# Transformer layer on one NeuronCore: TensorE makes each attention score one head further ahead

## What is computed

```
for i in blocks of 128 queries:                      # 8 row blocks
    s_loc = q_i . k[i-1, i, i+1] * scale, masked to |distance| <= 128
    s_ctx = q_i . k_ctx * scale
    p = softmax([sink, s_ctx, s_loc])
    o_i = p[ctx] @ v_ctx + p[loc] @ v[i-1, i, i+1]   # for each of 8 query heads
```

## Time and profile before

| | |
|---|---|
| median of 3 runs | 1198.11 us (1193.68 to 1208.54) |
| profiled execution | 1199.23 us, span 1197.4 us |
| PE busy | 1138.2 us (95%) |
| DVE busy | 936.9 us (78%) |
| ACT busy | 573.9 us (48%) |
| mean granted clock of TensorE | 0.981 |
| head groups (first turn to end of the last values) | 241.2 to 432.2 us |

### The profile page before, as it was taken

The page is one execution under the profiler, slowest core; times in us unless marked ns, Lnnn a source line. Parts: engine busy times, 40 slices in busy tenths (PEclk is TensorE's granted clock), DMA queues, the critical chain, the costliest instruction groups (busy, mean ns, idle before and its releaser), DMA issues.

```text
span 1197.4 us, 17074 instructions
## 1 busy us (share of the span) xinstructions
PE 1138.2 (95%) x5953; PEld 969.7 (81%) x5953; DVE 936.9 (78%) x1428; ACT 573.9 (48%) x981; POOL 290.2 (24%) x331
## 2 busy tenths in 40 slices
PE   7899999989898999998799999999999999999996
PEld 7778888889898887776688787878888878888885
DVE  1479988769897664469999999999999875867763
ACT  4362346756565765545444434344434444444441
POOL 2100011115455000002544545463600030000111
PEclk9999999979999999999899999999999999999998
DMA  9321555519999514212444453535333284443474
GB/s 368 132 76 62 128 102 110 114 64 223 251 264 256 151 53 158 106 69 89 155 162 152 146 175 123 175 123 175 123 122 105 88 298 159 115 115 96 119 165 69
DMA packets 103090, 171.77 MB, mean 143 GB/s; under 512 B 9322, under 2 KB 62690, under 8 KB 102004
## 3 DMA queue, kind: packets, MB, share of 16 engines
q1 hardware_dynamic: 82388, 104.70, 26.4%
q0 software_dynamic: 20640, 66.27, 23.5%
HBM read 112.21 MB, written 31.46 MB: 120 GB/s over the span
## 4 chain that ended last, share of the span: by engine, by line
PE 33%; DVE 16%; issue 8%; ACT 5%; DVEq 1%; ACTq 0%; POOL 0%
PE ps L1603 11%; PE ps L1653 6%; PE ps L1654 6%; PE ps L1655 6%; PE ps L1568 5%; DVE y L2016 4%; DVE w_op L1915 3%; DVE w_raw L1933 2%; DVE y L2012 2%; ACT w_op L1724 2%; ACT y L1804 2%; DVE u L2005 1%; DVE s_sum L1933 1%; ACT h_first L1717 0%; DVE scal L2047 0%
## 5 line engine op out<-in xcount | busy, mean ns | idle before, releaser
L1603 PE MATMUL ps<-t_op,w_op 128*128 128x512 f32 x1056 | 247.6, 390 | 3.2 <-DVE cv L2005 1.8
L1603 PEld LDWEIGHTS ps<-t_op,w_op 128*128 128x128 f32 x1056 | 197.6, 188 | 47.4 <-issue 4.3
L1603 PE MATMUL ps<-hx,w_op 128*128 128x512 f32 x792 | 192.4, 396 | 10.7 <-DVE u L2005 7.5
L1603 PEld LDWEIGHTS ps<-hx,w_op 128*128 128x128 f32 x792 | 150.8, 191 | 45.0 <-DVE u L2005 6.5
L1724 ACT ACTIVATE w_op<-w_raw 128x512 fp32r<-128x512 f32 x132 | 80.0, 623 | 199.5 <-DVE w_raw L1933 190.8
L1653 PE MATMUL ps<-dnh,ah 128*128 128x512 f32 x308 | 120.0, 390 | 1.6 <-DVE dnl L2023 1.6
L1655 PE MATMUL ps<-dnh,al 128*128 128x512 f32 x308 | 119.8, 389 | 0.0
L1654 PE MATMUL ps<-dnl,ah 128*128 128x512 f32 x308 | 119.8, 389 | 0.0
L1915 DVE TENSOR_TENSOR w_op<-w_raw,w_op 128x512 fp32r<-128x512 f32 x132 | 101.4, 782 | 10.0 <-ACT w_op L1724 8.2
L1824 ACT ACTIVATE ah<-hid 128x512 fp32r<-128x512 f32 x77 | 48.6, 632 | 116.7 <-PE ps L1655 112.7
L2023 DVE TENSOR_TENSOR al<-hid,ah 128x512 fp32r<-128x512 f32 x77 | 53.3, 692 | 48.8 <-ACT ah L1824 48.0
(11 more groups left out here) (287 smaller groups left out, 2393.3 us busy)
## 6 DMA issues: line engine op xcount, KB each, us to landing
w_raw<-in_w_up SPq DMA_DIRECT2D x44, 512.0 KB, 5.0
wm<-in_w_mod SPq DMA_DIRECT2D x32, 512.0 KB, 6.1
sums<-wm POOLq DMA_DIRECT2D x32, 512.0 KB, 8.4
wd<-in_w_down POOLq DMA_DIRECT2D x44, 256.0 KB, 3.3
w_down_sums<-wd POOLq DMA_DIRECT2D x44, 256.0 KB, 2.8
dn_raw<-w_down_sums SPq DMA_DIRECT2D x44, 256.0 KB, 2.6
hid_scratch<-hid SPq DMA_DIRECT2D x20, 512.0 KB, 4.2
hid<-hid_scratch POOLq DMA_DIRECT2D x20, 512.0 KB, 5.4
```

The lines of the kernel that those rows point to most:

```text
L1603: last = pe.matmul(bank_of(p, s), w_op[p][w][:, k, :], rows_of(p, k, v), start=(start and k == 0 and w == 0 and v == 0), stop=(k == KH - 1 ...
```

## The change

In head groups, TensorE makes the score of head hh = 4(n + 1) + j + 1 ahead of `turn(n, j)`, where it made that of head 4(n + 1) + j. So at j = 3 of group n it makes the first score of group n + 2. The very first place is as it was (two scores), the second, which was without, gets one, and groups 14 and 15 have one less and none. ScalarE's, VectorE's and the queues' lists are the same, and so are the banks and every wait inside `scores` and `turn`.

```diff
                         if (n, j) == (0, 0):
                             scores(1, 0)
-                            scores(1, 1)
-                        elif (n, j) != (0, 1) and n + 1 < NGRP and j < GQ:
-                            scores(n + 1, j)
+                        hh = GQ * (n + 1) + j + 1
+                        if j < GQ and hh < GQ * NGRP:
+                            scores(*divmod(hh, GQ))
                         turn(n, j)
```

## The result

The changed kernel took 1256.91 us (median of 4, 1254.34 to 1288.18) against 1196.36 us for the kernel before (4 runs, 1193.68 to 1208.54): ratio 1.0491, 95% interval 1.0447 to 1.0535. By the ratio it is 59 us slower, and the median lies outside the forecast range of 1211 to 1246. The highest run was a disturbed one and is left out of the ratio. The profiled execution took 1254.34 us, its span 1252.5 us.

A forecast was written before the change was run, and what follows sets the result against it. TensorE and VectorE were taken as close to full in the head groups, waiting mostly for each other. Terms of 20.6 + 1.5 + 3.5 + 3.0 = 28.6 us on 1199.23 gave 1227.8, stated as 1227.5 us, range 1211 to 1246.

The forecast's parts named there:

- That the groups are on the path, and nothing hides them: Behind the head groups TensorE runs without a gap, so a microsecond lost in them is one of the whole kernel.
- The closed chain: Head-group steps: turn, copy, exponential, score, next turn become one chain, 3.12 us against 2.23; eleven groups, +20.6 us.
- The sum of 28.6 us: Whole kernel: 20.6 us for eleven groups plus 1.5, 3.5 and 3.0 us, added to the profiled time.
- The smaller terms: Squares in groups 11 and 12 +1.5 us, groups 0 and 1 +3.5, groups 13 and 14 +3.0.
- The clock: Rival: idle of about 1.5 us per group brings half clock, 1.24 us in one step, 16 us in all; chance 0.20.
- What the profile would show: Scores (line 646) idle 40 to 50 times by about 0.9 us, once per group 1.5; VectorE's score waits near nothing.
- a shorter chain: Rival in the group steps: a step of 2.7 us, 15 us slower in all, about 1215 us; chance 0.14.
- VectorE setting the pace: Rival in the groups: the score's wait does not bite, a group takes 11.2 us, about 1187 us; chance 0.08.

The follow-up runs named there:

- The four-bank kernel: Changed kernel with four key tiles instead of five in groups 2 to 9 and scores there in four single banks: 1212.53 us, ratio 1.0118 to the kernel before.
- The kernel that keeps the full clock: Changed kernel plus 11 unread 128x256 matmuls behind turn 0 in groups 1 to 13: 1230.07 us, ratio 1.0285 to the kernel before.

## Why the prediction was wrong

- **That the groups are on the path, and nothing hides them**: right. Groups 2 to 12 lost 52.3 us and the span grew by 55.1 us.
- **The closed chain**: right, link by link (3.12 us forecast, 3.16 measured), and so was the group (14.15 against 14.25). The four-bank kernel and the one with the score behind the turn show it from two sides. The sum of 28.6 us was made for a full clock. The kernel that keeps the full clock has a profiled span 29.7 us above before's; its ratio of 1.0285 means 34 us, with an interval of 28 to 40.
- **The smaller terms**: not separable from the clock in the changed kernel. With the long idle filled, groups 0 and 1 cost 1.1 us more than before (forecast 3.5), groups 2 to 12 cost 23.7 (forecast 20.6 + 1.5) and groups 13 and 14 cost 5.9 (forecast 3.0, at most 4; the clock fell in group 14 behind an idle of 2.14 us). The total fits, in part because these misses cancel. The bounds of the terms add up to 1220 to 1233 us on the median, not to the 1218 to 1237 that the prediction gives.
- **The clock**: here the prediction failed. The sum has no term for it; it stood beside the sum as a rival of 16 us. I saw the trigger, named the place (the idle of 1.5 us behind turn 0, measured 1.55), and the price per step was right (1.24 us; measured 4.39 against 3.15). Two things were wrong. I held it unlikely, 0.20, on the argument that the turn and the score around the idle time are dense. The trace of before had no idle of that length between them, so nothing there bore the argument out, and it had a second case of the low clock that I did not use, behind an idle of 2.00 us:

```profile
362.18 1.10 PE L686 MATMUL ps<-vraw,pt 128*128 128x64 f32 x8 [2.00 <-ACT pt L989]
...
364.17 1.07 PE L674 MATMUL ps<-ident,p 128*128 128x128 f32 x4
```

And I let each idle time cost one step. The low clock did not come behind each, but where it came it lasted, once for about 31 us and once for 34 us on end: twelve steps of 4.4 us in groups 2, 3, 6, 7, 9 and 10, five more of 3.6 to 4.2 us in groups 2, 5, 6 and 9, and in groups 6 and 9 the group's end too (8.8 us from turn 3 to the next turn 0, against 4.8). That is 12 x 1.25 + 5 x 0.75 + 2 x 4.0 = 27 us. The measured price is the ratio of 1.0491 to 1.0285, 2.0% or about 25 us, where the rival had 16. Forecast and clock together, 1227.5 + 25, would have been 1253. What I had not thought of is that the short idle times, harmless alone, count beside the long one.
- The rule that I cited from the Trainium skill ("TensorE: Matmul & The Clock Gate", section on a second failure mode) describes such a case, short idle times between groups of matmuls that cycle through PSUM banks, and the trace agrees with it: clock 0.73 in the groups, and 1.00 once the long idle time in each is filled. I had weighed it by a single counterexample of 1.09 us, shorter than the idle at hand.
- **What the profile would show**: the idle before line 646 came, mostly 0.71 us (forecast 0.9) and 1.55 us, but 28 times and not 40 to 50. A group has two short ones beside the long one, not three, and at half clock TensorE's own work in a step (4.39 us) covers the chain. VectorE's waits for scores did not vanish: once TensorE is slower than VectorE, VectorE waits for it again.
- **The rivals on the other side** (a shorter chain, VectorE setting the pace) had no support: from group 1 on, no step of the changed kernel whose score has five key tiles was shorter than 3.1 us.

## What to carry to other kernels

Making work earlier in an in-order list moves its waits ahead of everything behind it. Before doing so, write down what the moved instruction waits for and whether that depends, through another engine, on what now stands behind it; with two buffers a lead of one closes such a loop, and the step becomes the sum of the links. Where an order leaves the matmul engine idle once in each round, look in the trace for the clock behind idle times of at least that length, count the shorter ones that the change adds beside it, and price a low clock by rounds, not by steps. If it cannot be excluded, forecast both and take the likelier from idle times as long as the new one, not from shorter ones. And where two kinds of idle are suspected, fill each alone and read the clock, not only the time.

## What the runs showed of the hardware

- Useless matmuls can pay. Eleven of 128x256 in an idle time of 1.55 us, once in each of 13 groups, raised the clock between 256 and 420 us from 0.73 to 1.00 and made the kernel about 2% faster.
- An idle time of 0.7 us in every step of 3.15 us, with the long one filled, left the clock at 1.00 from 256 to 420 us. With the long one there and the short ones filled it was 0.93 (0.99 from 290 us on, through eight long ones), with both there 0.73.
- An idle of about 1.55 us before a score was followed by a low clock in four of eight cases in the changed kernel, and in one of ten (1.5 to 1.8 us) in the kernel with the short ones filled.
- At the low clock TensorE was busy without a gap, 18.00 of 18 us from 389 to 407, and the granted clock stayed at 0.50 throughout.

```profile
389.00:407.00 18.00, 18.00 (x86) 17.72 (x86) 8.51 (x17) 5.46 (x12) 2.70 (x3) 0.50 0.66 184
```
